# The first layer's q projection and gates on x times the norm's weight, with the inverse rms applied at the eviction

## The reference, cut to what matters

```
h    = concat(meta_tokens, x)                        # 272 x 1024
y    = h * rsqrt(mean(h*h) + eps) * norm_mix[0]       # rmsnorm
proj = y @ w_in                                      # q (512), k (512), v, o (1024 each), 8 gates
q    = proj[q] * 128**-0.5
g    = 15 * tanh((proj[gates] + b_gate) / 15)        # 4 input gates, 4 forget gates
lf   = log_sigmoid(g[4:]);  cumulative sum and running maximum over the tokens follow
```

## Time and profile before

| | |
|---|---|
| three runs | 686.07, 682.2, 684.86 us; median 684.86 |
| the profiled execution | 684.74 us, of which the span is 683.0 |
| mean granted clock over the span | 0.973 |
| DVE, ACT and POOL busy | 204.7, 143.6 and 30.3 us |
| DMA | 150.05 MB, mean 220 GB/s over the span |

### The profile page before, as it was taken

One profiled execution on the slowest core, in us unless ns is written; L12 is line 12 of the kernel. 1 busy time (PEld: TensorE's weight loads), 2 busy tenths in 40 slices (PEclk: granted clock), 3 DMA queues, 4 the chain that ended last, 5 costly groups with the idle time before them and its releaser, 6 DMA issues.

```text
span 683.0 us, 7900 instructions
## 1 busy us (share of the span) xinstructions
PE 642.3 (94%) x3052; PEld 397.9 (58%) x3052; DVE 204.7 (30%) x588; ACT 143.6 (21%) x396; POOL 30.3 (4%) x60
## 2 busy tenths in 40 slices
PE   6889999999998899999988999999999889999994
PEld 3566877777774444554446777777767543334331
DVE  2323111222044234444353333333311521212201
ACT  1112012322141111111032333333212311111110
POOL 5000000000002000000001000000000300000000
PEclk9999899999999899999999999999999889999998
DMA  9997131013414999998996505020342389999921
GB/s 287 283 274 225 61 131 55 1 62 123 185 66 128 400 405 413 421 422 360 355 348 204 185 1 185 29 95 1 124 144 103 115 330 420 420 421 421 419 101 63
DMA packets 59114, 150.05 MB, mean 220 GB/s; under 512 B 10082, under 2 KB 42914, under 8 KB 46786
## 3 DMA queue, kind: packets, MB, share of 16 engines
q1 hardware_dynamic: 55554, 136.71, 53.7%
q0 software_dynamic: 2912, 10.64, 4.4%
q10 hardware_dynamic: 608, 2.16, 0.8%
HBM read 146.27 MB, written 3.23 MB: 219 GB/s over the span
## 4 chain that ended last, share of the span: by engine, by line
PE 89%; ACT 3%; DVE 3%; DMA 3%; issue 1%; ACTq 0%; SPq 0%; DVEq 0%
PE bank L1197 34%; PE bank L1431 18%; PE bank L1455 8%; PE bank L1470 5%; PE bank L1474 4%; PE bank L1413 3%; PE bank L1292 3%; DMA qk_area<-xs,idx 1%; PE bank L1206 1%; PE bank L1595 1%; PE bank L1582 1%; PE bank L1224 1%; PE bank L1624 1%; ACT tok L600 1%; PE bank L1328 1%
## 5 line engine op out<-in xcount | busy, mean ns | idle before, releaser
L1197 PE MATMUL bank<-xT,ring 128*128 128x272 f32 x640 | 157.1, 401 | 5.6 <-ACT qk_area L534 3.0
L1197 PEld LDWEIGHTS bank<-xT,ring 128*128 128x128 f32 x640 | 122.7, 195 | 32.6 <-issue 6.4
L1431 PE MATMUL bank<-ring,gate_area 128*64 128x512 f32 x512 | 120.5, 626 | 3.1 <-issue 2.6
L1431 PEld LDWEIGHTS bank<-ring,gate_area 128*64 128x64 f32 x512 | 38.1, 144 | 79.3 <-issue 79.2
L1197 PE MATMUL bank<-tok,ring 128*128 128x272 f32 (+1 forms) x256 | 60.9, 391 | 0.6 <-DVE tok L1181 0.6
L1455 PE MATMUL bank<-ring,gate_area 128*64 128x512 f32 x256 | 57.8, 593 | 0.0
L1197 PEld LDWEIGHTS bank<-tok,ring 128*128 128x128 f32 x256 | 47.4, 190 | 13.5 <-issue 6.1
L947 DVE TENSOR_TENSOR qk_area<-qk_area,bank 128x256 f32<-128x256 f32 x16 | 6.7, 421 | 119.4 <-ACT qk_area L642 119.4
L1455 PEld LDWEIGHTS bank<-ring,gate_area 128*64 128x64 f32 x256 | 18.4, 137 | 36.3 <-issue 36.3
L467 POOL DMA_INDIRECT qk_area<-xs,idx x16 | 17.8, 1114 | 456.7 <-DMA xs<-tok 329.6
L1470 PE MATMUL bank<-big 128*128 128x272 f32 x128 | 32.5, 399 | 1.2 <-DVE big L961 1.2
(11 more groups left out here) (243 smaller groups left out, 592.7 us busy)
## 6 DMA issues: line engine op xcount, KB each, us to landing
ring<-in_moe_w_gate SPq DMA_DIRECT2D x32, 1024.0 KB, 8.8
ring<-in_moe_w_up SPq DMA_DIRECT2D x32, 1024.0 KB, 11.5
ring<-in_moe_w_down SPq DMA_DIRECT2D x32, 1024.0 KB, 16.5
ring<-in_m_w_in SPq DMA_DIRECT2D x12, 1024.0 KB, 10.6
ring<-in_kv_w SPq DMA_DIRECT2D x8, 1024.0 KB, 11.8
ring<-in_m_w_out SPq DMA_DIRECT2D x4, 1024.0 KB, 10.8
ring<-in_f_w_q SPq DMA_DIRECT2D x4, 1024.0 KB, 8.4
ring<-in_f_w_o SPq DMA_DIRECT2D x4, 1024.0 KB, 5.1
```

Source lines behind the costliest of these rows:

```text
L1197: ins = pe.matmul(bank[c % 2][:, 0:n], w[:, k, half * P:half * P + P], x[:, k, 0:n], start=(k == 0), stop=(k == KB - 1))
L1431: ins = pe.matmul(bank[1][s, :], xgT[b % 2][:, q, s], ring[:, r:r + 2, q * FE:(q + 1) * FE], start=(q == 0), stop=(q == KB - 1))
```

## The change

- `hT[k]` times the gain (no rms) is made by ACT, one Copy with a per-partition scale for each block, into `sgoT`, which was free at that time. q's projections and the gates read `sgoT`. k, v and o still read `xT`, which DVE now makes as `sgoT` times `rsB`.
- The sum of squares is one output row (partition 64 of bank 4) and interleaved, block by block, with the gates' two chains (partitions 0 and 32 of the same bank), behind q's first projection. ACT copies that row out, PE spreads it over the partitions by one matmul (bank 5), and ACT makes `rsB` from it.
- q's evictions go from ACT to DVE (`queries`) and multiply by `rsB`. DVE multiplies the gates by `rsB` before ACT's Exp; the gates' bias enters as that Exp's bias.
- `grow` is transposed ahead of x. PE issues 14 matmuls of 128x128 by 128x128 on constants before its first wait for data.
- SP issues x's first tile and then the units. ACT's queue issues x's second tile, the meta tokens, `grow`, and the gates' weights and biases.

```diff
@@ sync
+            sp.dma_start(tok[:, 0, :], io["x"][0, 0:P, :]).then_inc(sem("x_loaded0"), 16)
@@ scalar
+            act.dma_start(tok[:, 1, :], io["x"][0, P:2 * P, :]).then_inc(sem("x_loaded1"), 16)
+            act.dma_start(tok[0:META, 2, :], io["meta_tokens"]).then_inc(sem("x_loaded2"), 16)
+            ... (grow x4, w_gates, b_gates: act.dma_start for sp.dma_start)
             load_exp_ln()
             act.wait_ge(sem("init_ready"), 1)
-            squares("norm0", 0, NT, lambda k: (sem("hT_in"), k + 1))
-            inverse_rms("norm0", 4, NT)
+            act.wait_ge(sem("gT_ready"), 1)
+            for k in range(KB):
+                act.wait_ge(sem("hT_in"), k + 1)
+                act.activation(sgoT[:, k, :], hT[:, k, :], ACT.Copy, scale=gT[:, MIX0 + k:MIX0 + k + 1]) \
+                    .then_inc(sem("xT_norm0"), 1)
+            squares("norm0", 0, NT, lambda k: (sem("hT_in"), KB))
+            act.wait_ge(sem("ssq_norm0"), KB)
+            act.activation(rsB[64:65, :], bank[4][64:65, 0:NT], ACT.Copy).then_inc(sem("rs_norm0"), 1)
+            act.wait_ge(sem("srow0_mm"), 1)
+            link(act.activation(rsB[:, :], bank[5][:, 0:NT], ACT.Ln, bias=eps_col[:, :], scale=1.0 / D))
+            act.activation(rsB[:, :], rsB[:, :], ACT.Exp, scale=-0.5).then_inc(sem("rs_norm0"), 1)
-            for j in range(PH["q0"]):
-                act.wait_ge(*done("proj", "q0", j + 1))
-                act.activation(qT[:, j, :], bank[j % 2][:, 0:NT], ACT.Copy, scale=MDK ** -0.5) \
-                    .then_inc(sem(f"proj_read{j % 2}"), 1)
@@ vector
-            dve.wait_ge(sem("rs_norm0"), 1)
-            normed("xT_norm0", xT, MIX0, 0)
+            def queries(j):
+                dve.wait_ge(*done("proj", "q0", j + 1))
+                dve.scalar_tensor_tensor(qT[:, j, :], bank[j % 2][:, 0:NT], MDK ** -0.5, rsB[:, :], ALU.mult, ALU.mult) \
+                    .then_inc(sem(f"proj_read{j % 2}"), 1)
+            dve.wait_ge(sem("small_loaded"), 16 * 2)
+            dve.tensor_scalar(b_gates[:, :], b_gates[:, :], 2.0 / GATE_CAP, None, ALU.mult)
+            dve.wait_ge(sem("rs_norm0"), 2)
+            queries(0)
+            dve.wait_ge(sem("gate_mm"), 1)
+            for a in (0, 1):
+                ins = dve.tensor_tensor(row_g[:, a * NT:(a + 1) * NT], bank[4][32 * a:32 * a + MH, 0:NT],
+                                        rsB[32 * a:32 * a + MH, :], ALU.mult)
+            ins.then_inc(sem("gate_z"), 1)
+            queries(1)
+            for k in range(KB):
+                dve.tensor_tensor(xT[:, k, :], sgoT[:, k, :], rsB[:, :], ALU.mult).then_inc(sem("xT_norm0"), 1)
+            queries(2)
+            queries(3)
@@ tensor
+            pe.wait_ge(sem("init_ready"), 1)
+            for _ in range(14):
+                pe.matmul(bank[7][:, 0:P], ones_f[:, :], ones_f[:, :], start=True, stop=True)
             pe.wait_ge(sem("ident_ready"), 1)
+            pe.wait_ge(sem("grow_loaded"), 16 * 4)
+            pe.transpose(bank[5][:, 0:48], grow[:, :], ident[0:48, 0:48]).then_inc(sem("gT_mm"), 1)
             ... (x is transposed as before)
-            sum_squares("norm0", 4, NT)
-            project("q0", 0, xT, NT, "xT_norm0")
+            project("q0", 0, sgoT, NT, "xT_norm0")
             pe.wait_ge(sem("small_loaded"), 16 * 2)
+            for k in range(KB):
+                pe.wait_ge(sem("sq_norm0"), k + 1)
+                pe.matmul(bank[4][64:65, 0:NT], ones_f[:, 0:1], colT[k % 2][:, :], start=(k == 0), stop=(k == KB - 1)) \
+                    .then_inc(sem("ssq_norm0"), 1)
+                for a in (0, 1):
+                    ins = pe.matmul(bank[4][32 * a:32 * a + MH, 0:NT], w_gates[:, k, MH * a:MH * (a + 1)], sgoT[:, k, :],
+                                    start=(k == 0), stop=(k == KB - 1))
+            ins.then_inc(sem("gate_mm"), 1)
+            project("q0", 1, sgoT, NT, k1=2)
             pe.wait_ge(sem("rs_norm0"), 1)
+            pe.matmul(bank[5][:, 0:NT], ones_f[64:65, :], rsB[64:65, :], start=True, stop=True).then_inc(sem("srow0_mm"), 1)
+            project("q0", 1, sgoT, NT, k0=2)
+            for j in range(2, 4):
+                project("q0", j, sgoT, NT)
+            pe.wait_ge(sem("xT_norm0"), 2 * KB)
             for j in range(4):
                 project("k0", j, xT, NT)
```

More of the change, by code:

```diff
@@ L78, in build @@
         dsqB, rstdB = [big[:, D + 256 + i * NT:D + 256 + (i + 1) * NT] for i in (MH, MH + 1)]
-        ones_row = rstdB[0:1, :]
         v1 = big[:, 3 * D:5 * D].rearrange("p (t d) -> p t d", t=2)
@@ L127, in build @@
         w_gates = sb("w_gates", [P, KB, 2 * MH])
-        b_gates = sb("b_gates", [1, 2 * MH])
+        b_gates = sb("b_gates", [MH, 2])
         w_f = sb("w_f", [P, KB, FH])
@@ L517, in inverse_rms @@
                 act.activation(rsB[:, 0:n], rsB[:, 0:n], ACT.Exp, scale=-0.5).then_inc(sem(f"rs_{name}"), 1)
+            act.dma_start(tok[:, 1, :], io["x"][0, P:2 * P, :]).then_inc(sem("x_loaded1"), 16)
+            act.dma_start(tok[0:META, 2, :], io["meta_tokens"]).then_inc(sem("x_loaded2"), 16)
+            with nc.allow_non_contiguous_dma(reason="small parameter vectors"):
+                for r, g in ((MIX0, io["norm_mix"].rearrange("l (k p) -> (l k) p", p=P)),
+                             (FFN0, io["norm_ffn"].rearrange("l (k p) -> (l k) p", p=P)),
+                             (KVN, io["kv_norm"].rearrange("(k p) -> k p", p=P)),
+                             (GOUT, io["m_g_out"][0].rearrange("h (j p) -> (h j) p", p=P))):
+                    n = 16 if r < KVN else 8
+                    act.dma_start(grow[r:r + n, :], g).then_inc(sem("grow_loaded"), 16)
+                act.dma_start(w_gates[:, :, :], w_in[:, 3072:3080].rearrange("(k p) c -> p k c", k=KB)) \
+                    .then_inc(sem("small_loaded"), 16)
+                act.dma_start(b_gates[:, :], io["m_b_gate"][0].rearrange("(a h) -> h a", a=2)) \
+                    .then_inc(sem("small_loaded"), 16)
@@ L519, in _ @@
             load_exp_ln()
             act.wait_ge(sem("init_ready"), 1)
-            squares("norm0", 0, NT, lambda k: (sem("hT_in"), k + 1))
-            inverse_rms("norm0", 4, NT)
-            act.wait_ge(sem("gate_mm"), 1)
+            act.wait_ge(sem("gT_ready"), 1)
[3 more added lines that the diff above has]
+                    .then_inc(sem("xT_norm0"), 1)
@@ new lines, in _ @@
+            squares("norm0", 0, NT, lambda k: (sem("hT_in"), KB))
[4 more added lines that the diff above has]
+            act.activation(rsB[:, :], rsB[:, :], ACT.Exp, scale=-0.5).then_inc(sem("rs_norm0"), 1)
+            act.wait_ge(sem("gate_z"), 1)
@@ L525, in _ @@
             for a in (0, 1):
-                ins = act.activation(row_g[:, a * NT:(a + 1) * NT], bank[4][32 * a:32 * a + MH, 0:NT], ACT.Exp,
-                                     scale=2.0 / GATE_CAP)
+                ins = act.activation(row_g[:, a * NT:(a + 1) * NT], row_g[:, a * NT:(a + 1) * NT], ACT.Exp,
+                                     scale=2.0 / GATE_CAP, bias=b_gates[:, a:a + 1])
             ins.then_inc(sem("gate_e"), 1)
@@ L733, in _ @@
             dve.memset(tok4[:, :, :], 0.0)
-            dve.memset(ones_row, 1.0)
             dve.memset(ones16[:, :], 1.0).then_inc(sem("init_ready"), 1)
+            dve.wait_ge(sem("gT_mm"), 1)
+            dve.tensor_copy(gT[:, :], bank[5][:, 0:48]).then_inc(sem("gT_ready"), 1)
             for k in range(KB):
@@ L739, in _ @@
                 dve.tensor_copy(hT[:, k, :], bank[2 + k % 2][:, 0:NT]).then_inc(sem("hT_in"), 1)
-            dve.wait_ge(sem("gT_mm"), 1)
-            dve.tensor_copy(gT[:, :], bank[5][:, 0:48]).then_inc(sem("gT_ready"), 1)
-            dve.wait_ge(sem("gT_ready"), 1)
             def normed(name, dst, g, c0, ready=None):
@@ L1226, in _ @@
                 ins.then_inc(sem("x_tr"), 1)
-            pe.wait_ge(sem("grow_loaded"), 16 * 4)
-            pe.transpose(bank[5][:, 0:48], grow[:, :], ident[0:48, 0:48]).then_inc(sem("gT_mm"), 1)
-            sum_squares("norm0", 4, NT)
-            project("q0", 0, xT, NT, "xT_norm0")
+            project("q0", 0, sgoT, NT, "xT_norm0")
             pe.wait_ge(sem("small_loaded"), 16 * 2)
-            pe.wait_ge(sem("rs_norm0"), 1)
[L1234 to L1243, removed]
+            for k in range(KB):
[7 more added lines that the diff above has]
+            project("q0", 1, sgoT, NT, k1=2)
+            pe.wait_ge(sem("rs_norm0"), 1)
+            pe.matmul(bank[5][:, 0:NT], ones_f[64:65, :], rsB[64:65, :], start=True, stop=True).then_inc(sem("srow0_mm"), 1)
[3 more added lines that the diff above has]
+            pe.wait_ge(sem("xT_norm0"), 2 * KB)
             for j in range(4):
```

## The result

Ten runs of the changed kernel have a median of **680.44 us** (677.51 to 681.5), ten of the kernel before 684.74 (682.2 to 686.09). The ratio is 0.9929, 95% interval 0.9912 to 0.9945: 4.3 us faster by the medians, where 10.8 were forecast and 671 to 679.5 was the range. The direction was right, the size 2.5 times too large.

The account below looks back on a forecast made before the run. PE was taken to bound the kernel, with 89% of the span's chain of waits. The steps moved the end of k's projections from 60.83 to 50.0, 10.8 us off the median 684.86: 674.0 us, range 671 to 679.5.

Parts of the forecast that it names:

- Start of the data: Before the transpositions: x, meta tokens and `grow` landed at 7.0 us, between 6.2 and 9.0.
- PE's 14 matmuls: Matmuls on constants before PE's first data: from about 1.4 us, ending between 5.0 and 8.6, taken near 7.0.
- The transpositions, 4.4: PE's transpositions of x after `grow`'s, at 2.4 GHz: 4.4 us for eight blocks, ending at 11.7.
- q's first projection, 5.2: PE after transposing x: 3.9 us at 2.4 GHz plus 1.3 for a lost clock, ending at 16.9.
- Rival (a): Clock at 1.2 GHz through transpositions and most of q's first projection: 4.1 us more, 678.1 us; chance 0.19.
- Sums beside the gates, 5.4: After q's first projection: sums of squares and gate chains side by side in 5.4 us, ending at 22.3.
- rival (b): Sums of squares and gates run one after the other: 5.6 us more, 679.5 us; chance 0.09.
- The new wait, 1.6: Within k's projections, at about 41 us: PE waits 1.6 us for bank 0, for DVE's eviction behind the gate chain.
- The sum to the end of k: All steps up to the end of k's projections: 50.0 us instead of 60.83, 10.8 us gained.
- Each stretch moves as a whole: After k's projections: order unchanged, stretches only move earlier; the clock's falls may shift by 2 us either way.
- rival (d): ACT's small loads stand behind SP's eight units: `grow` lands near 26, PE starts 19 us late, 693 us; chance 0.03.

## Why the prediction was wrong, step by step

- **Start of the data: the step that failed.** "I take 7.0"; it was 9.12, and 8.97 in both further profiles, at the upper bound of 9.0. Two things were mis-sized. ACT's issues of `grow` took 0.28 to 0.66 us, not the 0.33 of the earlier trace rows, a row of other loads 200 us later; the last one came at 3.62 and not at 2.9. The kernel before had the nearer row, the last of the same four issues on SP's queue:

```profile
3.50 0.27 SPq L347 DMA_DIRECT2D grow<-in_m_g_out  x1
```

  SP's issues of units beside it add 0.36: where SP waits, ACT's last is at 3.26. And it landed 5.37 later. The row that gave the upper bound, small loads among units, was the near one, the meta tokens' row the far one: what is asked for first had been made last in a loaded queue.
- **PE's 14 matmuls: the term that was missing.** They were put to end "near 7.0 as well", together with the data. They ended at 6.47 and the data came at 9.12. No price was put on a pause between the two, though the earlier trace rows show one (34 to 37 us) with its fall of the clock behind it. Here it costs 2.2 + 1.4 = 3.6 us (26 matmuls against 14), on top of the 2.1 us of waiting. The forecast already held 1.3 of it, for q's first projection and for another reason.
- **The transpositions, 4.4:** right (4.5) in the seven kernels where the matmuls come right before them or at most 1.58 us ahead; 6.67 in the changed one, with 2.66 us between.
- **q's first projection, 5.2:** measured 5.25, which is luck: the number is right for another reason than the one given. I read from the earlier trace rows that transpositions lose the clock. They don't raise it (kernel before), but with matmuls close ahead the clock stayed at 2.4 GHz through all 4.5 us of them (7.50 to 12.00, PEclk 1.00), and q's projection took 3.9. The rule of the Trainium skill ("TensorE: Matmul & The Clock Gate", Part 4), that a transposition does not count as busy, fits the first and not the second. Rival (a) named the right symptom at 678.1: 7.0 us for the transpositions, with `grow`'s, was measured as 6.98. The other half of its 4.1 us, 7.0 for q's first projection, did not come; the late start, which it didn't have, made up the sum.
- **Sums beside the gates, 5.4:** 4.6 (21.35 to 25.97). The chains do run beside each other, as two rows of the changed kernel's timeline show (start, duration), and rival (b) falls:

```profile
21.28 0.39 PE L1258 MATMUL bank<-colT,ones_f 128*1 128x272 f32 x1
...
21.29 0.40 PE L1261 MATMUL bank<-gate_area,w_gates 128*4 128x272 f32 x2
```

- **The new wait, 1.6:** 1.43 (bank 0, released by DVE's eviction of k at L789), as described. With one queue it is 1.71, and 1.8 us of chain went with it.
- **The sum to the end of k:** 2.1 for the start, 2.3 for the transpositions, 0.1 for q's first, - 0.8 for the sums, and 0.7 for what follows (28.4 for 27.7, mostly the spreading matmul and q's second projection) are, before rounding, the 4.35 by which 54.35 misses 50.0. The 60.83 of the other side is one execution's too: 59.3 to 60.8 in four profiles of the kernel before, mostly by whether the clock fell behind the pause at 34 us.
- **"Each stretch moves as a whole":** nearly. No wait on units appeared, and rival (d) did not come (`grow` landed at 9, not at 26). But the clock's falls, allowed for as 2 us either way, went mostly one way: against the kernel before, each of the eleven other kernels loses 1.9 to 2.4 us of its lead at one or both of the experts' entries. In the changed kernel's first profile the lead is 6.5 us at the end of k, 7.6 at the heads, 7.7 at the first expert's transposition, 5.7 at its down projection and 5.8 at the end; its median is another 1.3 us behind that profile. Of the 6.5 us by which the medians miss the forecast (4.3 for 10.8), 4.35 are thus made before 54.35 and about 2 behind it. The part after 60 us is observed, its cause is not shown.

## What to carry to other kernels

Warm-up matmuls have to reach close to the first real work (2.2 us short of it lost the clock here, 1.6 us short did not): count when the last transfer it waits for lands in a loaded queue, and rather issue too many (26 for 14 gained 3 us, 18 for 14 cost nothing). When work is reordered so that a small load is needed first, its place in the queues has to move too; a second queue brought nothing here (1.0005) and made the last small load late. An operation that goes to another engine takes the waits ahead of it there along: k's evictions behind the gate chain cost 1.4 to 1.7 us, and moving them to ACT returned it.

## What the runs showed of the hardware that was not expected

- In the first microseconds the clock column can say 1.00 while PE works at 1.2 GHz: the kernel before has 1.00 for 6.50 to 13.30 with a block of transpositions in 0.83 us, while at a true 1.00 it takes 0.56 (one queue, 7.50 to 12.00).
- A pause of PE of 2.2 to 2.7 us ahead of the transpositions (the changed kernel's three profiles, and `grow` first) went with a fall to 1.2 GHz for about 10 us; pauses of 0.79, 1.10 and 1.58 us there did not, and one of 1.4 to 1.7 us for bank 0 was not followed by a fall at once. The length alone doesn't settle it. The kernel before pauses for 2.96 us at 34 us in all four profiles; in three the clock falls within 1.1 us of the pause's end, in the fourth it doesn't. Nor does it in the kernel before with two queues, whose six projections take 22.24 us for the 23.93 of the earlier trace rows:

```profile
37.40 22.24 PE bank L1197 x96
```

- The clock fell while PE was busy without a gap (4.00 of 4.00 us for 48 to 52, then the fall at 52.5), in a loop of float32 matmuls with four rows and eight of 128x128 among them. The eight lengthened the loop by 3.0 us (9.15 from k's end to v's start for 6.18), where back to back at full clock they take 2.05; here they took 3.7, in part at 1.2 GHz.
